# Strassen's seven products for the down projections of two MLPs, over all eight PSUM banks in turn

## The chip, the core and the metric

The kernel runs on one NeuronCore of a Trainium2 chip, as one launch. The metric is the device time of that launch in microseconds (us), the median of several runs. Engines are named as in the profile: PE (TensorE, the matrix engine), PEld (its weight loads), DVE (VectorE), ACT (ScalarE), POOL (GpSimd), SP (SyncE, which issues the loads of weights).

## What is computed

Two transformer-like blocks on one sequence of 1024 tokens with 1024 channels, in float32. What the change touches is the MLP at the end of each block:

```
u = rmsnorm(h, norm_mlp_g[l]) @ w_up[l]
h = h + jnp.square(jax.nn.relu(u)) @ w_down[l]
```

`w_up` is 1024 x 4096 and `w_down` 4096 x 1024. The second block has the same MLP with weights of its own, and a norm behind it that ends the kernel. The rest (dilated attention and a convolution, cross attention to 256 memory rows, a gated linear recurrence, neighbourhood attention) is the same before and after.

## The kernel before

All activations lie transposed, channels on the 128 partitions: `H` is 8 blocks of 128 channels x 1024 tokens. A float32 product is made of three passes of a faster 4-byte format: each operand is split into a high part that the format holds exactly and a low remainder, and hi*hi, hi*lo and lo*hi are summed in PSUM. PE's `job(q, s, x)` (L420) is one output block of 128 channels x 1024 tokens: for 8 inner blocks k, three passes, two halves of 512 tokens, 48 matmuls of 128x512, all recorded at L435. It fills `PJ[s]`, two of the eight PSUM banks; `PX` (four banks) is used by norms and attention, and stands unused in the MLPs. Job number 2q+s counts through the whole program, `s` alternating; semaphore `products` counts finished jobs.

The weights of a job come as one 512 KB tile into `raw[:, s]` by SP (`load`, L277). POOL's `split(q, s)` waits until the tile is there and until job 2q+s-2 has ended (its slot of `w_hi`/`w_lo` is then free), runs a one-column operation (L360), copies the high part (`w_hi`, L361) and subtracts for the low part (`w_lo`, L366), and raises `w_split`, for which PE waits at the job's start and SP before it loads the slot again. DVE empties the bank pair: in an up job with the ReLU and the norm's scale into `T[s]` (L1559), in a down job by an addition to `H` (`take`, L1284); either raises `free[s]`, for which PE waits two jobs on.

In an MLP, 32 up jobs make 32 inner blocks of 128, and the down projection needs all of them for each of 8 outputs. It goes in 4 chunks (`FF_CHUNKS`): 8 up jobs, then 8 down jobs over those 8 inner blocks. ACT squares `T[s]` twice, into the high part (L1076) and in place (L1077), and DVE subtracts for the low part (L1561). The chunks are hardware loops on PE, DVE, ACT and POOL. Ahead of the MLP, a norm: PE sums squares with `norm_stats` (L463) between the first two jobs, ACT takes the root (L878) and DVE the reciprocal `rstd` (`norm_std`, L1300), which the first eviction at L1559 needs. In the second MLP the last 8 down jobs are cut in halves of 512 tokens and written out by hand (L838), one bank for 24 matmuls, so that the last norm can begin early.

## Time and profile before

| | |
|---|---|
| median of 3 runs | 3181.73 us (3178.7 to 3182.39) |
| the profiled execution | 3180.11 us, its span 3178.3 us |
| PE busy | 3104.9 us, 98% of the span, 14982 matmuls |
| DVE / POOL / ACT busy | 43% / 33% / 25% |
| granted TensorE clock, mean | 0.994 |
| DMA | 61 GB/s over the span |
| the chain that ended last | PE 88%, of it L435 72% |

The span is cut into groups of instructions by line; a line of the chain of waits says what ended last at each moment. Matmuls overlap in the records, so that the mean duration of one (390 ns) is longer than the distance from one to the next; that distance is read from long pieces of the chain.

### The profile page before, as it was taken

How to read it: one execution, taken by the hardware profiler on the slowest of the kernel's cores; microseconds unless marked ns; L12 is line 12 of the kernel's file. 1: busy time of each engine (PE TensorE's matmuls, PEld its weight loads, DVE VectorE, ACT ScalarE, POOL GpSimd, SP SyncE). 2: the span in 40 equal slices, each digit the busy share in tenths (PEclk: the TensorE clock that was granted, in tenths of full speed). 3: DMA queues.
4: the chain of work that ended last, by engine and by line, in shares of the span. 5: the costliest groups of instructions: out<-in, count | busy, mean ns of one | idle time of the engine just before them, and what ended most of it. 6: DMA issues, size and time to landing. Idle time of an engine off the chain costs nothing.

```text
span 3178.3 us, 39032 instructions
## 1 busy us (share of the span) xinstructions
PE 3104.9 (98%) x14982; PEld 2464.2 (78%) x14982; DVE 1358.6 (43%) x1391; ACT 791.0 (25%) x1113; POOL 1052.2 (33%) x879
## 2 busy tenths in 40 slices
PE   8999999998999999999999999999999999999997
PEld 6776677875888888888767777887678888888886
DVE  7988874435331211113556566123775311111124
ACT  3005772114220101002243534112642201011011
POOL 3333323330333333333323333333353333333350
PEclk9999999999999999999999999999999999999999
DMA  3110002130111111111312121423131111111121
GB/s 138 47 40 33 2 28 86 47 119 7 47 46 47 53 47 46 53 46 46 112 50 80 61 74 53 165 71 130 37 126 47 46 53 47 47 50 50 46 67 53
DMA packets 50074, 194.16 MB, mean 61 GB/s; under 512 B 5680, under 2 KB 6320, under 8 KB 48560
## 3 DMA queue, kind: packets, MB, share of 16 engines
q1 hardware_dynamic: 43776, 152.50, 15.2%
q10 hardware_dynamic: 6192, 40.14, 3.3%
q8 instruction: 80, 1.31, 0.2%
q14 instruction: 26, 0.21, 0.0%
HBM read 171.12 MB, written 21.50 MB: 61 GB/s over the span
## 4 chain that ended last, share of the span: by engine, by line
PE 88%; DVE 7%; DMA 1%; ACT 1%; issue 1%; POOL 1%; SPq 0%; ACTq 0%; DVEq 0%; POOLq 0%
PE psum L435 72%; PE psum L838 3%; DVE cacc L1313 2%; PE psum L710 2%; PE psum L532 2%; PE psum L518 2%; PE psum L547 2%; DMA raw<-weights 1%; PE psum L771 1%; PE psum L785 1%; PE psum L758 1%; PE psum L661 1%; PE psum L641 1%; PE psum L497 0%; DVE rstd L1300 0%
## 5 line engine op out<-in xcount | busy, mean ns | idle before, releaser
L435 PE MATMUL psum<-A_hi,w_hi 128*128 128x512 f32 x2176 | 680.4, 394 | 18.3 <-DVE A_lo L1290 13.2
L435 PE MATMUL psum<-A_lo,w_hi 128*128 128x512 f32 x2176 | 671.5, 390 | 0.0
L435 PE MATMUL psum<-A_hi,w_lo 128*128 128x512 f32 x2176 | 671.0, 389 | 0.0
L360 POOL TENSOR_TENSOR small<-ident 128x1 f32<-128x1 f32 x250 | 63.0, 252 | 1813.3 <-PE psum L435 1781.9
L366 POOL TENSOR_TENSOR w_lo<-raw,w_hi 128x1024 fp32r<-128x1024 f32 x234 | 591.8, 2529 | 19.5
L435 PEld LDWEIGHTS psum<-A_hi,w_hi 128*128 128x128 f32 x2176 | 408.4, 188 | 113.5 <-issue 27.4
L435 PEld LDWEIGHTS psum<-A_lo,w_hi 128*128 128x128 f32 x2176 | 409.4, 188 | 85.5
L435 PEld LDWEIGHTS psum<-A_hi,w_lo 128*128 128x128 f32 x2176 | 409.1, 188 | 85.7
L435 PE MATMUL psum<-B_hi,w_hi 128*128 128x512 f32 x1472 | 454.9, 390 | 3.1 <-POOL w_lo L366 2.0
L435 PE MATMUL psum<-B_hi,w_lo 128*128 128x512 f32 x1472 | 453.2, 389 | 0.0
L435 PE MATMUL psum<-B_lo,w_hi 128*128 128x512 f32 x1408 | 433.6, 389 | 0.0
L1284 DVE TENSOR_TENSOR H<-psum,H 128x1024 f32 x80 | 98.0, 1225 | 562.2 <-PE psum L435 561.4
L435 PEld LDWEIGHTS psum<-B_hi,w_hi 128*128 128x128 f32 x1472 | 276.0, 188 | 62.4 <-POOL w_lo L366 2.4
L435 PEld LDWEIGHTS psum<-B_hi,w_lo 128*128 128x128 f32 x1472 | 276.3, 188 | 57.6
L435 PEld LDWEIGHTS psum<-B_lo,w_hi 128*128 128x128 f32 x1408 | 264.3, 188 | 54.9
L361 POOL TENSOR_SCALAR w_hi<-raw 128x1024 fp32r<-128x1024 f32 x250 | 264.4, 1058 | 0.0
L1559 DVE SCALAR_TENSOR_TENSOR t<-psum,rstd 128x1024 f32<-128x1024 f32 x64 | 78.4, 1225 | 374.7 <-PE psum L435 373.5
L1313 DVE SCALAR_TENSOR_TENSOR cacc<-U,par,cacc 128x1009 f32<-128x1009 f32 (+14 forms) x120 | 173.7, 1448 | 3.3
L1076 ACT ACTIVATE A_hi<-t 128x1024 f32 x32 | 34.0, 1062 | 531.9 <-DVE t L1559 531.9
L1076 ACT ACTIVATE B_hi<-t 128x1024 f32 x32 | 34.0, 1062 | 531.9 <-DVE t L1559 531.9
L384 POOL TENSOR_SCALAR P<-P,small 128x1024 f32<-128x1024 f32 x64 | 72.0, 1138 | 128.3 <-DVE small L1405 128.3
L1284 DVE TENSOR_TENSOR t<-psum,rstd 128x1024 f32<-128x1024 f32 x38 | 46.5, 1225 | 120.9 <-PE psum L435 117.2
(237 smaller groups left out, 3025.1 us busy)
## 6 DMA issues: line engine op xcount, KB each, us to landing
raw<-weights SPq DMA_DIRECT2D x256, 512.0 KB, 3.5
gate_spill<-RU SPq DMA_DIRECT2D x16, 512.0 KB, 3.1
H<-x ACTq DMA_DIRECT2D x2, 2048.0 KB, 8.6
x_spill<-H ACTq DMA_DIRECT2D x1, 4096.0 KB, 11.1
R<-gate_spill ACTq DMA_DIRECT2D x8, 512.0 KB, 4.5
mixed_spill<-t ACTq DMA_DIRECT2D x8, 512.0 KB, 2.9
BE<-rel_bias ACTq DMA_DIRECT2D x8, 512.0 KB, 4.4
MIX<-mixed_spill ACTq DMA_DIRECT2D x1, 4096.0 KB, 15.3
```

Of the source, the lines that this page charges most:

```text
L361: hi = pool.tensor_scalar(w_hi[:, s], raw[:, s], 1.0, 1.0, ALU.mult, ALU.mult)
L366: pool.tensor_tensor(w_lo[:, s], raw[:, s], f32(w_hi[:, s]), ALU.subtract).then_inc(S["w_split"], 1)
L384: pool.tensor_scalar(probs[:], probs[:], rsums[p % 3][:, h:h + 1], 1.0, ALU.mult, ALU.mult).then_inc(S["probs"], 1)
L435: last = pe.matmul(PJ[s][:, c:c + step], w[:, s, k, :], b[:, k, c:c + step], start=(k == 0 and i == 0), stop=(k == kblocks - 1 and i == 2))
L518: last = pe.matmul(to[h][:, c:c + HALF], Q[rows, m, P * t:P * t + P], K[rows, m, c:c + HALF], start=True, stop=True)
L532: last = pe.transpose(PX[:, HALF * (part % 2) + P * k:HALF * (part % 2) + P * k + P], P1[h][p % 3][:, key:key + P], ident[:])
L547: last = pe.matmul(PX[DH * h:DH * h + DH, 1024 + P * t:1024 + P * t + P], V[:, k, 2 * DH * m + DH * h:2 * DH * m + DH * h + DH], PT1[h][p ...
L838: last = pe.matmul(fin_bank(n), w, x[:, k, half_of(h)], start=(k == 0 and i == 0), stop=(k == KB - 1 and i == 2))
L1076: tallies["u_hi"](act.activation(block_of(u[0], m), T[s][:], ACT.Square))
L1284: dve.tensor_tensor(out, PJ[s], in1, op).then_inc(free[s], 1)
L1313: done(dve.scalar_tensor_tensor(cacc[:, a:b], u(a + sh, b + sh), w, cacc[:, a:b], ALU.mult, ALU.add))
L1559: dve.scalar_tensor_tensor(T[s][:], PJ[s], 0.0, rstd[:], ALU.max, ALU.mult).then_inc(free[s], 1)
```

## The change

In each MLP, 24 of the 32 inner blocks (6 groups of 4) go through the down projection by Strassen's scheme, in the form with seven products. Its blocks are: two output blocks 2j and 2j+1, two halves of the group's inner blocks (two blocks each), and two halves of 512 tokens. One new unit `("down", g, j)`, a *pair* in what follows, is 7 products of 6 matmuls (2 inner blocks x 3 passes) where the plain way needs 48 matmuls; each group has 4 pairs. Each product fills one bank of its own, and DVE adds the seven banks to `H` in six additions (`add_pair`), which raise `st_read` or `free`; PE waits for these before it fills a bank again. `H` is changed to differences of its blocks at the MLP's start and back at the end of the pairs (`rebase`, two operations on 4x512 columns each time). The last 8 inner blocks go the plain way.

The operands of the products: DVE and ACT make seven activations per two inner blocks, each in a high and a low part (`combine` on DVE, `split_group` on ACT; into `XS`, which lies where the squared activations lay). DVE makes four sums of weights per pair (`weight_sums`, 4 operations on 256 columns), into one buffer `WS`; POOL splits the three weight quarters that are used as they are (`split_pair`) and then `WS`. The order of the units is the table `FF_UNITS`: four up jobs; then per group two up jobs, four pairs, two up jobs (u u d d d d u u); up jobs 26 to 31; the 8 plain down jobs. The unit count stays 64. All of it is straight-line code but the last down jobs of the first MLP. POOL also waits for the norm's sums before it splits unit 2, since some of its new buffers lie in `acc`.

The core of the diff (the low parts of the last 8 blocks, the table of weights made on the host and the semaphores' names are left out):

```diff
+GROUPS = 6
+def ff_units():
+    units = [("up", t) for t in range(4)]
+    for g in range(GROUPS):
+        units += [("up", 4 * g + 4), ("up", 4 * g + 5)] + [("down", g, j) for j in range(4)]
+        if g < GROUPS - 1:
+            units += [("up", 4 * g + 6), ("up", 4 * g + 7)]
+    return units + [("up", t) for t in range(26, 32)] + [("last", m) for m in range(KB)]
+FF_UNITS = ff_units()
...
+        XS = [at(f"XS{l}", (o_b, o_a)[l], [7, 2, 2, HALF], F32R) for l in range(2)]
...
+        WS = at("WS", o_t + 2 * KIB4, [KB, P])
...
-            splits(ROUNDS["xo"], ROUNDS["qkv2"] + 6)
+            def split_pair(q, s, layer):
+                pool.wait_ge(raw_in[s], 16 * q + 16)
+                pool.wait_ge(S["products"], 2 * q + s - 1)
+                pool.tensor_tensor(small[:, 12:13], ident[:, 0:1], ident[:, 0:1], ALU.mult)
+                hi12, lo12 = W12[layer][s]
+                hi22, lo22 = W22[layer][s]
+                chain(pool.tensor_scalar(hi12[:], raw[:, s, 0:4], 1.0, 1.0, ALU.mult, ALU.mult))
+                chain(pool.tensor_scalar(hi22[:], raw[:, s, 6:8], 1.0, 1.0, ALU.mult, ALU.mult))
+                chain(pool.tensor_tensor(lo12[:], raw[:, s, 0:4], f32(hi12[:]), ALU.subtract))
+                chain(pool.tensor_tensor(lo22[:], raw[:, s, 6:8], f32(hi22[:]), ALU.subtract))
+            def split_units(name, layer, end):
+                pool.wait_ge(S["stats"], 3 + 2 * layer)
+                pairs = 0
+                for at_unit in range(2, end):
+                    unit, q, s = FF_UNITS[at_unit], ROUNDS[name] + at_unit // 2, at_unit % 2
+                    if unit[0] != "down":
+                        split(q, s)
+                        continue
+                    split_pair(q, s, layer)
+                    pairs += 1
+                    pool.wait_ge(S["st_weights"], 4 * GROUPS * layer + pairs)
+                    chain(pool.tensor_scalar(w_hi[:, s], WS[:], 1.0, 1.0, ALU.mult, ALU.mult))
+                    pool.tensor_tensor(w_lo[:, s], WS[:], f32(w_hi[:, s]), ALU.subtract).then_inc(S["w_split"], 1)
+            splits(ROUNDS["xo"], ROUNDS["ff"])
+            split(ROUNDS["ff"], 0)
+            split(ROUNDS["ff"], 1)
+            split_units("ff", 0, len(FF_UNITS))
+            splits(ROUNDS["rec_in"], ROUNDS["qkv2"] + 6)
...
+            def fast_down(q, s, layer, g, j):
+                pair = 4 * GROUPS * layer + 4 * g + j
+                wait_split(pe, q, s, "late")
+                if j == 0:
+                    pe.wait_ge(S["st_lo"], 2 * GROUPS * layer + 2 * g + 2)
+                w12, w22 = W12[layer][s], W22[layer][s]
+                sums = (w_hi[:, s], w_lo[:, s])
+                def product(bank, w, at_w, x):
+                    for i in range(2):
+                        for t, (a, b) in enumerate(((0, 0), (0, 1), (1, 0))):
+                            last = pe.matmul(bank, w[a][:, at_w + i, :], XS[layer][:, x, b, i, :],
+                                             start=(i == 0 and t == 0), stop=(i == 1 and t == 2))
+                    return last
+                if pair > 1:
+                    pe.wait_ge(S["st_read"], 3 * pair - 5)
+                product(PX[:, HALF * (j % 2):HALF * (j % 2) + HALF], w12, 0, 0).then_inc(S["st_done"], 1)
+                if pair:
+                    pe.wait_ge(S["st_read"], 3 * pair - 1)
+                product(PX[:, 1024:1024 + HALF], w12, 2, 1)
+                product(PX[:, 1024 + HALF:2048], sums, 2, 6).then_inc(S["st_done"], 1)
+                if j == 0:
+                    pe.wait_ge(free[0], q)
+                else:
+                    pe.wait_ge(S["st_read"], 3 * pair)
+                product(PJ[0][:, 0:HALF], sums, 4, 4).then_inc(S["st_done"], 1)
+                product(PJ[0][:, HALF:SEQ], w22, 0, 5).then_inc(S["st_done"], 1)
+                pe.wait_ge(free[1 - s], q + s)
+                product(PJ[1][:, 0:HALF], sums, 6, 2)
+                product(PJ[1][:, HALF:SEQ], sums, 0, 3).then_inc(S["products"], 1)
             def mlp(name, x, u, n, layer):
                 q0 = ROUNDS[name]
-                u_ready = lambda c: (S["u_lo"], [8 * c + (32 * layer + k + 1) for k in range(KB)])
-                rounds(q0, 4, x, stats=norm_stats(n), ready=norm_ready(n))
-                rounds(q0 + 4, 4, u, ready=u_ready(0))
-                with pe.Fori(1, FF_CHUNKS - layer) as c:
-                    for i in range(4):
-                        for s in range(2):
-                            job(8 * c + (q0 + i), s, x)
-                    for i in range(4):
-                        for s in range(2):
-                            job(8 * c + (q0 + 4 + i), s, u, ready=u_ready(c) if i == 0 and s == 0 else None)
+                job(q0, 0, x, ready=norm_ready(n))
+                norm_stats(n)()
+                for at_unit in range(1, len(FF_UNITS) - 8):
+                    unit, q, s = FF_UNITS[at_unit], q0 + at_unit // 2, at_unit % 2
+                    if unit[0] == "up":
+                        if FF_UNITS[at_unit - 1][0] == "down":
+                            pe.wait_ge(S["st_read"], 3 * (4 * GROUPS * layer + 4 * FF_UNITS[at_unit - 1][1] + 4))
+                        job(q, s, x)
+                    else:
+                        fast_down(q, s, layer, *unit[1:])
+                if layer == 0:
+                    rounds(q0 + 28, 4, u, ready=(S["u_lo"], [k + 1 for k in range(KB)]))
...
+                def split_group(c):
+                    i = c % 2
+                    x = XS[layer]
+                    at_h = lambda p: x[:, p:p + 2, 0, i, :]
+                    halves = lambda t: t[:].rearrange("p (a b) -> p a b", a=2)
+                    tallies["st_hi"](act.activation(x[:, 0, 0, i, :], T[0][:, 0:HALF], ACT.Copy))
+                    tallies["st_hi"](act.activation(at_h(1), halves(T[1]), ACT.Copy))
+                    for t in range(2):
+                        act.wait_ge(S["st_sum"], 4 * GROUPS * layer + 2 * c + t + 1)
+                        tallies["st_hi"](act.activation(at_h(3 + 2 * t), halves(T[t]), ACT.Copy))
...
+                def combine(c):
+                    i = c % 2
+                    left, right = slice(0, HALF), slice(HALF, SEQ)
+                    halves = lambda t: t[:].rearrange("p (a b) -> p a b", a=2)
+                    minus = lambda out, a, b: chain(dve.tensor_tensor(out, a, b, ALU.subtract))
+                    done = 4 * (2 * GROUPS * layer + c)
+                    dve.wait_ge(S["st_hi"], done + 1)
+                    dve.tensor_tensor(x[:, 0, 1, i, :], T[0][:, left], f32(x[:, 0, 0, i, :]), ALU.subtract)
+                    dve.wait_ge(S["st_hi"], done + 2)
+                    chain(dve.tensor_tensor(x[:, 1:3, 1, i, :], halves(T[1]), f32(x[:, 1:3, 0, i, :]), ALU.subtract))
+                    minus(T[0][:, left], T[0][:, right], T[0][:, left])
+                    tl["st_sum"](dve.tensor_tensor(T[0][:, right], T[1][:, right], T[0][:, right], ALU.subtract))
+                    minus(T[1][:, right], T[1][:, right], T[0][:, left])
+                    tl["st_sum"](dve.tensor_tensor(T[1][:, left], T[1][:, left], T[1][:, right], ALU.subtract))
+                    dve.wait_ge(S["st_hi"], done + 3)
+                    dve.tensor_tensor(x[:, 3:5, 1, i, :], halves(T[0]), f32(x[:, 3:5, 0, i, :]), ALU.subtract)
+                    dve.wait_ge(S["st_hi"], done + 4)
+                    tl["st_lo"](dve.tensor_tensor(x[:, 5:7, 1, i, :], halves(T[1]), f32(x[:, 5:7, 0, i, :]), ALU.subtract))
...
+                def weight_sums(g, j):
+                    at_unit = units_of[("down", g, j)]
+                    q, s = q0 + at_unit // 2, at_unit % 2
+                    dve.wait_ge(raw_in[s], 16 * q + 16)
+                    if 4 * g + j:
+                        before = units_of[("down", g, j - 1) if j else ("down", g - 1, 3)]
+                        wait_split(dve, q0 + before // 2, before % 2, "late")
+                    k = lambda a: raw[:, s, 2 * a:2 * a + 2]
+                    to = lambda a: WS[:, 2 * a:2 * a + 2, :]
+                    chain(dve.tensor_tensor(to(0), k(2), k(3), ALU.add))
+                    dve.tensor_tensor(to(2), k(0), k(2), ALU.subtract)
+                    chain(dve.tensor_tensor(to(1), to(0), k(0), ALU.subtract))
+                    tl["st_weights"](dve.tensor_tensor(to(3), k(1), to(1), ALU.subtract))
+                def add_pair(q, s, g, j):
+                    pair = 4 * GROUPS * layer + 4 * g + j
+                    both = lambda half: H[:, 2 * j:2 * j + 2, half_of(half)]
+                    banks = lambda t, n=2: t.rearrange("p (a b) -> p a b", a=n)
+                    dve.wait_ge(S["st_done"], 4 * pair + 1)
+                    twice = banks(PX[:, HALF * (j % 2):HALF * (j % 2) + HALF], 1).to_broadcast([P, 2, HALF])
+                    tl["st_read"](dve.tensor_tensor(both(0), twice, both(0), ALU.add))
+                    dve.wait_ge(S["st_done"], 4 * pair + 2)
+                    tl["st_read"](dve.tensor_tensor(both(0), banks(PX[:, 1024:2048]), both(0), ALU.add))
+                    for n in range(2):
+                        dve.wait_ge(S["st_done"], 4 * pair + 3 + n)
+                        out = H[:, 2 * j + 1, half_of(0)]
+                        chain(dve.tensor_tensor(out, PJ[0][:, half_of(n)], out, ALU.add))
+                    tl["st_read"](dve.tensor_tensor(both(1), both(1), banks(PJ[0]), ALU.subtract))
+                    wait_job(dve, q, s)
+                    dve.tensor_tensor(both(1), banks(PJ[1]), both(1), ALU.add).then_inc(free[s], 1)
+                def rebase(forward):
+                    even, odd = H[:, 0:KB:2, :], H[:, 1:KB:2, :]
+                    steps = [(even[:, :, HALF:SEQ], odd[:, :, HALF:SEQ]), (odd[:, :, HALF:SEQ], odd[:, :, 0:HALF])]
+                    for out, other in steps if forward else steps[::-1]:
+                        chain(dve.tensor_tensor(out, out, other, ALU.subtract if forward else ALU.add))
+                rebase(True)
+                for at_unit in range(len(FF_UNITS) - 8):
+                    unit, q, s = FF_UNITS[at_unit], q0 + at_unit // 2, at_unit % 2
+                    if unit[0] == "down":
+                        g, j = unit[1:]
+                        add_pair(q, s, g, j)
+                        if j < 2:
+                            weight_sums(g, j + 2)
+                        if j == 3:
+                            if g < GROUPS - 1:
+                                combine(2 * g + 2)
+                            else:
+                                dve.wait_ge(free[s], q + 1)
+                                rebase(False)
+                                low(0)
+                                low(1)
+                        continue
+                    t = unit[1]
+                    evict(q, s)
+                    if t < 4 * GROUPS:
+                        if t == 1 or t % 4 == 3:
+                            dve.wait_ge(S["st_sq"], 4 * GROUPS * layer + t + 1)
+                            combine(t // 2)
+                    elif t >= 4 * GROUPS + 2:
+                        low(t - 4 * GROUPS)
+                    if t >= 4 and t % 4 < 2 and t <= 4 * GROUPS + 1:
+                        weight_sums(t // 4 - 1, t % 4)
```

How the order of instructions moves, at three places. PE, a down job in the first MLP of before (the waits of an instruction in brackets; the first rows of 16 like them):

```order
L435 MATMUL psum<-B_hi,w_hi 128x512 [waits free1,w_split]
L435 MATMUL psum<-B_hi,w_hi 128x512
L435 MATMUL psum<-B_lo,w_hi 128x512 x2
L435 MATMUL psum<-B_hi,w_lo 128x512 x2
L435 MATMUL psum<-B_hi,w_hi 128x512 x2
```

The second pair of a group in the change, from its first row to the fourth product (`W_010` and `W_011` are a weight quarter's high and low part):

```order
L746 MATMUL psum<-XS_131,W_010_135 128x512 [waits w_split]
L746 MATMUL psum<-XS_131,W_010_135 128x512
L746 MATMUL psum<-XS_131,W_011_136 128x512
...
L746 MATMUL psum<-XS_131,W_010_135 128x512 [waits st_read]
...
L746 MATMUL psum<-XS_131,w_hi 128x512 [waits st_read]
...
L746 MATMUL psum<-XS_131,w_hi 128x512 [waits free0]
```

Where a job waited at its start alone, a pair also waits ahead of its second, fourth and sixth product. POOL, the work for one job of before:

```order
L360 TENSOR_TENSOR small<-ident 128x1 [waits products,raw1]
L361 TENSOR_SCALAR w_hi<-raw 128x1024
L366 TENSOR_TENSOR w_lo<-raw,w_hi 128x1024 [waits pool_chain]
```

And for one pair in the change:

```order
L420 TENSOR_TENSOR small<-ident 128x1 [waits products,raw1]
L423 TENSOR_SCALAR W_010_135<-raw 128x512
L424 TENSOR_SCALAR W_010_143<-raw 128x256 [waits pool_chain]
L425 TENSOR_TENSOR W_011_136<-raw,W_010_135 128x512 [waits pool_chain]
L426 TENSOR_TENSOR W_011_144<-raw,W_010_143 128x256 [waits pool_chain]
L439 TENSOR_SCALAR w_hi<-WS 128x1024 [waits st_weights,pool_chain]
L440 TENSOR_TENSOR w_lo<-WS,w_hi 128x1024 [waits pool_chain]
```

The old two stand at its end, behind DVE's sums (`st_weights`), and four new ones ahead of them. On DVE the six additions of a pair are one of 1024 columns behind the first product, one of 1024 behind the third, one of 512 behind the fourth and the fifth each, one of 1024 (which frees `PJ[0]`), and one of 1024 behind the last. In the first two pairs of a group the four sums for the pair after the next follow the sixth addition; behind the fourth pair comes `combine`. DVE at the start of the first MLP, before:

```order
L1296 TENSOR_TENSOR acc<-acc,t_61 128x1024 [waits norm_sq,norm_lo]
L112 REGISTER_ALU [waits norm_acc]
L112 COMPARE_AND_BRANCH
L1300 RECIPROCAL rstd<-rstd 128x1024 [waits std]
L112 UNCONDITIONAL_BRANCH [waits dve_chain]
L112 UNCONDITIONAL_BRANCH
L112 ISA
L1559 SCALAR_TENSOR_TENSOR t_59<-psum,rstd 128x1024 [waits products]
```

And in the change:

```order
L1409 TENSOR_TENSOR acc<-acc,t_61 128x1024 [waits norm_sq,norm_lo]
L128 REGISTER_ALU [waits norm_acc]
L128 COMPARE_AND_BRANCH
L1413 RECIPROCAL rstd<-rstd 128x1024 [waits std]
L1739 TENSOR_TENSOR H<-H 128x4x512 [waits dve_chain] x2
L1672 SCALAR_TENSOR_TENSOR t_59<-psum,rstd 128x1024 [waits products,dve_chain]
```

The two operations of `rebase` stand between the reciprocal and the first eviction, where before no work stood.

## Rows read from the trace of the kernel before

**Rows 1.** The page: each engine's busy time, share of the span, instructions

```profile
PE 3104.9 (98%) x14982; PEld 2464.2 (78%) x14982; DVE 1358.6 (43%) x1391; ACT 791.0 (25%) x1113; POOL 1052.2 (33%) x879
```

**Rows 2.** Chain that ended last: start us, us, what; MLPs, last down jobs

```profile
875.41 696.36 PE psum L435 x3072
...
2473.28 598.46 PE psum L435 x2640
...
3127.60 32.70 PE psum L838 x144
```

**Rows 3.** Busy by windows, first MLP: PE, PEld, DVE, ACT, POOL, clock, DMA

```profile
875.00:1571.00 696.00, 696.00 (x3071) 576.09 (x3071) 161.24 (x123) 97.82 (x105) 230.89 (x190) 1.00 0.16 50
```

**Rows 4.** Timeline of POOL in the first MLP: start us, us, what

```profile
887.77 3.25 POOL L366 TENSOR_TENSOR w_lo<-raw,w_hi 128x1024 fp32r<-128x1024 f32 x1
...
908.25 0.20 POOL L360 TENSOR_TENSOR small<-ident 128x1 f32<-128x1 f32 x1 [7.25 <-PE psum L435]
908.40 1.05 POOL L361 TENSOR_SCALAR w_hi<-raw 128x1024 fp32r<-128x1024 f32 x1
909.54 2.40 POOL L366 TENSOR_TENSOR w_lo<-raw,w_hi 128x1024 fp32r<-128x1024 f32 x1
```

**Rows 5.** Timeline of DVE at the first MLP's start

```profile
876.60 6.55 DVE L1300 RECIPROCAL rstd<-rstd 128x1024 f32<-128x1024 f32 x1 [7.60 <-ACT rstd L878]
883.66 1.23 DVE L1559 SCALAR_TENSOR_TENSOR t<-psum,rstd 128x1024 f32<-128x1024 f32 x1 [0.50 <-DVE rstd L1300]
887.34 1.42 DVE L1561 TENSOR_TENSOR B_lo<-t,B_hi 128x1024 f32 x1 [2.45 <-ACT t L1077]
888.88 1.23 DVE L1559 SCALAR_TENSOR_TENSOR t<-psum,rstd 128x1024 f32<-128x1024 f32 x1
```

**Rows 6.** Groups by line and shape: busy us, mean ns, idle before

```profile
L1765 DVE TENSOR_TENSOR H<-psum,H 128x512 f32<-128x512 f32 x16 | 11.1, 692 | 43.4 <-PE psum L838 43.3
L1699 DVE COPY PT<-psum 128x256 f32<-128x256 f32 x64 | 27.1, 423 | 7.9 <-PE psum L771 7.7
L401 POOL TENSOR_SCALAR P<-P,small 128x512 f32<-128x512 f32 x32 | 21.8, 695 | 44.9 <-DVE small L1691 44.9
L1077 ACT ACTIVATE t<-t 128x1024 f32<-128x1024 f32 x64 | 68.1, 1063 | 2.0
```

**Rows 7.** DVE's evictions from PSUM: count, ns min/median/max, first and last start

```profile
L1284 DVE TENSOR_TENSOR H<-psum,H x80: 1224/1225/1225, 486.1 to 2984.8; 128x1024 f32 x80
...
L1559 DVE SCALAR_TENSOR_TENSOR t<-psum,rstd x64: 1224/1225/1226, 883.7 to 3071.8; 128x1024 f32<-128x1024 f32 x64
```

**Rows 8.** Timeline of POOL behind the second attention

```profile
2340.11 3.44 POOL L366 TENSOR_TENSOR w_lo<-raw,w_hi 128x1024 fp32r<-128x1024 f32 x1
```

**Rows 9.** Timeline of DVE, same stretch

```profile
2340.06 1.23 DVE L1740 TENSOR_TENSOR t<-t,MIX 128x1024 f32<-128x1024 f32 x1
2341.32 3.30 DVE L1732 TENSOR_TENSOR A_lo<-t,A_hi 128x1024 fp32r<-128x1024 f32 x1
```

**Rows 10.** Timeline of PE after a wait of 2.48 us

```profile
487.45 1.19 PE L435 MATMUL psum<-A_hi,w_hi 128*128 128x512 f32 x2 [2.48 <-DVE H L1284]
488.44 1.05 PE L435 MATMUL psum<-A_lo,w_hi 128*128 128x512 f32 x2
489.29 1.05 PE L435 MATMUL psum<-A_hi,w_lo 128*128 128x512 f32 x2
```

**Rows 11.** Busy by windows: after that wait, and after one of 5.0 us

```profile
487.00:490.00 3.00, 2.55 (x6) 2.10 (x7) 1.40 (x2) 2.30 (x3) 1.77 (x1) 0.55 0.15 19
...
3076.00:3126.00 50.00, 49.70 (x220) 40.82 (x219) 16.33 (x20) 5.71 (x9) 22.35 (x12) 1.00 0.18 53
```

**Rows 12.** Chain: the wait of 5.0 us that ended at 3076.78

```profile
3059.94 11.80 PE psum L435 x52
...
3076.78 49.96 PE psum L838 x219
```

More of the change, by code:

```diff
@@ L814, in _ @@
             mlp("ff2", B, A, 4, 1)
-            for i in range(4):
-                for s in range(2):
-                    job(LAST - 4 + i, s, B)
             for n in range(2 * KB):
@@ L831, in _ @@
                     if n == 0:
[L832 removed]
+                        pe.wait_ge(S["u_lo"], KB + k + 1)
                     if m < 2:
@@ L1563, in mlp, with evict @@
[L1563 to L1568 removed]
+                x = XS[layer]
+                sums_made = [0]
+                def evict(q, s):
+                    wait_job(dve, q, s)
+                    dve.scalar_tensor_tensor(T[s][:], PJ[s], 0.0, rstd[:], ALU.max, ALU.mult).then_inc(free[s], 1)
```

79 lines of the change are left out of this document (49 added, 30 removed).

## The prediction, written before the changed kernel was run

> **What bounds the kernel now.** I read the page first: PE is busy for 3104.9 of 3178.3 us [rows 1], so only fewer or shorter matmuls, or the few gaps, can make this kernel faster. Then the chain that ended last: the first MLP stands in it as one unbroken piece, 3072 matmuls in 696.36 us; the second, up to its last down jobs, as 2640 in 598.46 us [rows 2]. Both give 0.2267 us from one matmul to the next, job changes, loop ends and waits included. So a job of 48 is 10.88 us and six matmuls are 1.36 us. The windows show how far the others are from binding there: in 696 us DVE works 161, ACT 98, POOL 231 [rows 3]. POOL's work for a job is 0.20 + 1.05 + 2.40 us with gaps of 0.09, 3.8 us of 10.88, and begins when the job two back has ended [rows 4].
>
> **What the change removes.** A pair has 42 matmuls where 48 stood: 6 x 48 pairs = 288 fewer, x 0.2267 = **-65.3 us**. All of it lies on PE's path, since nothing else ends last in either MLP [rows 2]. The kernel has no other row for this count; the pair's matmuls have the same shape, and each its own weight load, as before (PE and PEld have the same count [rows 1]). The Trainium skill (TensorE: Matmul & The Clock Gate, "Back-to-back issue gap") gives 512/2.4 + 2.5 ns, 216 ns, for such a matmul at full clock. By it the saving would be 62.2 us; this trace has 226.7 ns for the 4-byte format, and I use that.
>
> **A bank for each six matmuls.** The nearest row is the written-out end of the second MLP, one bank per 24 matmuls: 144 in 32.70 us [rows 2], 0.05 us more than 144 x 0.2267 for six bank changes. At 0.008 us each, 336 products would cost 2.8 us. A job change in the loops costs nothing. I take 0, and keep 2.8 for the range; it also bounds what straight-line code costs against loops.
>
> **POOL, the closest margin.** For the second, third and fourth pair of a group it has 7 x 1.36 = 9.52 us, from the start of the pair before. Its ordinary pieces: 0.20; one-source operations of 512 and 256 columns at 0.70 [rows 6] and, on the line through 0.70 and 1.05 for 1024 [rows 4], 0.52; two-source ones on the line from 0.20 (1 column) to 2.40 (1024), 1.30 and 0.75; then WS at 1.05 + 2.40. With six gaps of 0.09 that is 7.5 us. DVE's four sums (256 columns, 0.43 each by [rows 6], 1.7 us) come 1.3 to 2 us after the start and must be done before WS is split. They have both inputs in SBUF, and such a DVE operation and POOL's exclude one another: at 2340 us DVE's operation runs its normal 1.23, POOL's takes 3.44 in place of 2.40, and DVE's next, queued behind it, 3.30 [rows 8, 9]; the same at 887 us, with 3.25 on POOL [rows 4, 5]. If nothing at all overlaps, 7.5 + 1.7 = 9.2 us: still 0.3 us before PE needs it. I put the likely end at 8.8 to 9.0 and the cost at **0**. The first pair of a group is made beside an up job (10.88 us) and has more room; an up job's 3.8 us fits anywhere.
>
> **DVE.** A pair's additions are 4 x 1.23 + 2 x 0.69 = 6.3 us [rows 6, 7] of 9.52. None of them is stretched by POOL: an operation with one PSUM input never took more than 1.226 us [rows 7], also at 888.88, in the middle of POOL's stretched one [rows 4, 5]. With the sums in front (done at about 5.2) the additions of the second and third pair end 11.5 us after their pair's start, that is 2.0 us into the next. PE needs `PX` again 1.36 us into the next pair (read at 7.7), `PJ[0]` 4.1 us in (read at 10.3, 0.8 in) and `PJ[1]` 6.8 us in. So every bank is free in time: **0**. The fourth pair has no sums before its additions, so the up job behind it finds `PJ[0]` read. `combine` with its ACT part is a chain of 1.23 (eviction) + 1.06 (square) + 1.66 (copies) + 1.23 + 4 x 0.69 + 1.06 + 1.23 = 10.2 us [rows 6, 7] against up jobs of 10.88; POOL may stretch it by 1 to 2.4 us. What is late then is the next eviction, and PE wants that bank only 10.88 us later: 0. Per group of 81.6 us DVE has 51 us, POOL 45, ACT 12. The slots of `raw` are filled again after `w_split`, some 9 us before they are read; SP's queue has nothing new in it.
>
> **The start of each MLP.** The reciprocal ends at 883.15 and the first eviction began at 883.66 [rows 5]. PE finishes the second job 10.88 us after 875.41, at 886.29, and its third needs the eviction's end (884.9 before, so no wait). `rebase` puts two operations of 2048 columns ahead of it: on the line through 0.69 for 512 and 1.23 for 1024 some 2.3 each [rows 6, 9]. First eviction over at 883.2 + 4.6 + 1.3 = 889.1: PE waits 2.8 us, twice **+5.6 us**. Lower bound 0 (if PE's order had more slack than I see), upper 2 x (2.8 + 1.0 for one of them held up by POOL). A wait can also halve the clock: after one of 2.48 us, in a stretch with others, the granted clock was 0.55 over 3 us and the distance 0.425 us [rows 10, 11], costing eight matmuls 0.2 each; after one of 5.0 us behind dense work it stayed 1.00 [rows 11, 12]. The MLP's start is dense, like the second: 0, with 2 x 1.6 in the range. `rebase` back (4.6 us) lies beside up job 26, and POOL's wait for the norm's sums delays the split of unit 2 by 1.7 us of some 7 spare: both 0.
>
> **The sum.** -65.3 + 5.6 = -59.7. The profiled execution took 3180.1 us around its span of 3178.3, so 3120.4; the median shown is 1.6 above it: **3122.0 us**.
>
> **Rivals.** (a) POOL is late. For: the margin is 0.3 to 0.7 us, and its small operations have no rows. Against: even the sum without any overlap fits. If a pair's weights come 0.4 to 1.1 us late, 36 pairs (three per group) cost 14 to 40 us: 3136 to 3162.
> (b) DVE is late: its sums wait behind several of POOL's operations, WS's 2.40 us among them, and the additions behind them run over. A wait of 1 to 2 us in two pairs per group, 24 pairs, costs 24 to 48 us: 3146 to 3170. Against: `PJ[0]` has 3.3 us to spare.
> (c) It gets slower: PE pauses briefly at the product changes, each with a wait and a fresh bank, and the clock falls. Place: the 2016 matmuls of the pairs. Price: 0.425 - 0.2267 = 0.198 us for each at half clock [rows 10]. It decides from 59.7 / 0.198 = 302 of them, 15% or six per pair; eight per pair, as in rows 10, would be 76 us: 3198. Against: 64 jobs with a wait at each lost nothing [rows 2]. The Trainium skill names just this (the same page, "A second HAM failure mode: psum-queue depth-cycling"): cycling through banks lets PE idle briefly between groups and its clock swing between the two levels. By that rule the change would lose its gain; the trace has no bank cycling this fast, so it can't refute it.
> (d) The saving isn't there. The order of instructions has 42 matmuls per pair, so I give this nothing of its own.
>
> **How the numbers follow.** Forecast 0.74, (a) 0.13, (b) 0.05, (c) 0.05; 0.03 is left for what I don't see. About 0.2% (6 us) is what a measurement here can tell from no change. The forecast, (a) and (b) are all faster: 0.92; (c) makes 0.05 slower; the rest lies between. Range: low end, no wait at the MLPs' start and a little noise, 3181.7 - 65.3 - 1 = 3115. The forecast's own costs reach to 3122.0 + 2.8 + 2.0 + 3.2 = 3130; the range goes on through most of (a), to 3150.
>
> **What would show it.** Each pair 9.5 us on PE; no wait of PE for `w_lo` or for an addition to `H` inside the pairs; two waits near 2.8 us for DVE at the third job of each MLP; clock at 1.00; WS's low part over some 0.5 us before the pair starts. Waits for L440 speak for (a), waits for L1723 to L1732 for (b), a clock below 1 in the MLPs' windows for (c). The forecast is wrong if PE's chain in the MLPs has gaps of more than 10 us together.

## The result, and the profile of the changed kernel

The change takes 3123.02 us in the median of 4 runs (3119.3 to 3126.63), beside 3181.14 us for the kernel before (4 runs, 3178.7 to 3182.39). The ratio is 0.9818, 95% interval 0.9801 to 0.9835: 58 us faster, and 1 us from the forecast of 3122. The terms behind the forecast were not all of that quality, as the rows show.

The page of the changed kernel: its span, each engine's busy time with the share of the span and the instructions, the granted clock in 40 slices, and the two largest of its three groups of the new products. They answer to [rows 1].

```profile
span 3117.5 us, 38588 instructions
...
PE 3039.6 (98%) x14694; PEld 2411.0 (77%) x14694; DVE 1906.4 (61%) x1975; ACT 830.9 (27%) x1161; POOL 1213.1 (39%) x1071
...
PEclk9999999999999999999999999999999999999999
...
L746 PE MATMUL psum<-XS,w_hi 128*128 128x512 f32 x768 | 236.4, 389 | 0.0
...
L746 PE MATMUL psum<-XS,W 128*128 128x512 f32 x864 | 211.4, 389 | 0.0
```

288 matmuls are gone (14982 to 14694). That PE's busy time fell by 65.3 us (3104.9 to 3039.6), just the first term, is in part chance. In the first MLP it fell by 30.8 us (696.4 to 665.6), in the second, up to its last down jobs, by 30.7 (598.4 to 567.7), since the slow restart described below takes back 1.9 us of each saving; the other 3.8 us lie where the change does nothing. The first term is read from the chain below. DVE's share rose from 43% to 61% and POOL's from 33% to 39%, and the last column of the products' groups says what that cost PE: its idle time before them is 0.0. So PE still bounds the kernel, and the question is where the other 5 to 7 us of the 65 went.

The chain that ended last in the changed kernel, first MLP (start us, us, what), answers to [rows 2]:

```profile
870.89 1.73 PE psum L517 x4
...
872.65 1.12 ACT rstd L964
...
873.80 6.56 DVE rstd L1413
...
880.38 2.30 DVE H L1739
...
882.71 2.30 DVE H L1739
...
885.04 1.23 DVE t L1672
...
886.41 45.41 PE psum L489 x192
931.81 38.08 PE psum L746 x168
969.89 43.52 PE psum L489 x192
...
1377.89 163.20 PE psum L489 x720
```

Read it from the end. Six groups of four pairs take 38.08 us each, 9.52 us a pair, and 38.08 / 168 = 0.2267 us a matmul: waits and bank changes of the pairs cost nothing that can be read. The up projections between them are at 43.52 / 192, again 0.2267. One piece differs: the first 192 matmuls take 45.41 us. Ahead of them stands what the single piece of [rows 2] did not have: the chain leaves PE and goes through the norm on ACT and DVE, the two halves of the rebase (L1739) and the first eviction (L1672), before PE goes on at 886.41. PE waits there, once in each MLP. Its waits (us in all, how many, longest):

```profile
PE psum L489 <- DVE t L1672: 5.7, 2, 2.9
```

Two stretches of the first MLP by engine (PE, PEld, DVE, ACT, POOL, then the granted clock, the DMA share and GB/s):

```profile
886.40:1541.00 654.60, 654.59 (x2881) 541.88 (x2882) 421.68 (x411) 116.91 (x128) 306.74 (x283) 1.00 0.16 53
...
887.00:890.00 3.00, 3.00 (x10) 2.35 (x9) 1.08 (x2) 2.87 (x4) 1.54 (x1) 0.64 0.06 8
```

From the wait to the MLP's end PE is busy without a break. Just behind the wait, from 887 to 890 us, the granted clock is 0.64: part of that time TensorE ran at 1.2 GHz in place of 2.4, and the 192 matmuls cost 45.41 - 43.52 = 1.9 us more. Behind the same wait at full clock, which three runs below show, they take 43.80 us; so 1.6 us of the 1.9 are the clock's and 0.3 us belong to the restart. One start thus costs 2.9 + 1.9 = 4.8 us, the second MLP's too (45.40 us for its first 192), 9.5 us together.

The account of the two profiled executions, 3180.1 against 3119.3 us, -60.8: the first MLP went from 696.36 to 668.47 us (872.62 to 1541.09), -27.9 = -32.6 + 4.8. The second MLP and what follows it gave -28.2, the same sum with 0.3 us of noise. The remaining -4.7 us lie ahead of the first MLP (its norm sums end at 872.62, before at 875.41) and between the MLPs (901.5 to 899.6), where the change does nothing; the experiments show this scatter too.

### The profile page after: what moved, and what is told of

The parts are those of the page before. It is cut to its first block, busy times and chain, and to the rows that moved or that the text cites. A ratio compares the mean times of both kernels' runs of the same rounds, so it can differ in the third digit from the quotient of the medians.

```text
span 3117.5 us, 38588 instructions
## 1 busy us (share of the span) xinstructions
PE 3039.6 (98%) x14694; PEld 2411.0 (77%) x14694; DVE 1906.4 (61%) x1975; ACT 830.9 (27%) x1161; POOL 1213.1 (39%) x1071
## 4 chain that ended last, share of the span: by engine, by line
PE 87%; DVE 8%; ACT 2%; issue 1%; DMA 1%; POOL 1%; SPq 0%; ACTq 0%; DVEq 0%; POOLq 0%
PE psum L489 56%; PE psum L746 15%; PE psum L924 3%; DVE cacc L1426 2%; PE psum L799 2%; PE psum L572 2%; PE psum L586 2%; PE psum L601 2%; PE psum L860 1%; PE psum L874 1%; PE psum L847 1%; PE psum L715 1%; DVE rstd L1413 1%; DMA raw<-weights 1%; PE psum L695 1%
## 5 line engine op out<-in xcount | busy, mean ns | idle before, releaser
L489 PE MATMUL psum<-A_hi,w_hi 128*128 128x512 f32 x1792 | 562.9, 395 | 21.7 <-DVE A_lo L1403 13.6
L489 PE MATMUL psum<-A_lo,w_hi 128*128 128x512 f32 x1792 | 553.5, 390 | 0.0
L489 PE MATMUL psum<-A_hi,w_lo 128*128 128x512 f32 x1792 | 553.1, 390 | 0.0
L489 PEld LDWEIGHTS psum<-A_hi,w_hi 128*128 128x128 f32 x1792 | 336.6, 189 | 102.3 <-issue 30.7
L489 PE MATMUL psum<-B_hi,w_hi 128*128 128x512 f32 x1088 | 337.8, 392 | 4.5 <-DVE t L1672 2.9
L489 PE MATMUL psum<-B_hi,w_lo 128*128 128x512 f32 x1088 | 335.5, 390 | 0.0
L489 PE MATMUL psum<-B_lo,w_hi 128*128 128x512 f32 x1024 | 315.8, 390 | 0.0
L1672 DVE SCALAR_TENSOR_TENSOR t<-psum,rstd 128x1024 f32<-128x1024 f32 x64 | 78.2, 1224 | 265.5 <-PE psum L489 263.9
L746 PE MATMUL psum<-XS,w_hi 128*128 128x512 f32 x768 | 236.4, 389 | 0.0
L746 PE MATMUL psum<-XS,W 128*128 128x512 f32 x864 | 211.4, 389 | 0.0
L746 PEld LDWEIGHTS psum<-XS,W 128*128 128x128 f32 x864 | 162.2, 188 | 33.6
L746 PEld LDWEIGHTS psum<-XS,w_hi 128*128 128x128 f32 x768 | 144.2, 188 | 29.9
```

The source lines that it names most:

```text
L489: last = pe.matmul(PJ[s][:, c:c + step], w[:, s, k, :], b[:, k, c:c + step], start=(k == 0 and i == 0), stop=(k == kblocks - 1 and i == 2))
L746: last = pe.matmul(bank, w[a][:, at_w + i, :], XS[layer][:, x, b, i, :], start=(i == 0 and t == 0), stop=(i == 1 and t == 2))
L1672: dve.scalar_tensor_tensor(T[s][:], PJ[s], 0.0, rstd[:], ALU.max, ALU.mult).then_inc(free[s], 1)
```

## Experiments

Each was timed in 3 or 5 rounds beside the kernel before; ratios are against the runs of before on the same chip. Its medians there were 3179.91 us (beside c0, e1, e3 and e4), 3179.5 us (beside e2, e5, e6 and e7) and 3181.77 us (beside e8 and e1b). The base c0 belongs to the first group, so that a difference from it in another group also holds what the kernel before differs by, 0.4 us for the second.

### The change again, as the base (c0)

> The change again, unaltered, as the measure for the others of this group. Theory: a median near 3123 us, as before (288 matmuls fewer, -65.3, and two waits at the starts of the MLPs with the clock's fall behind them, +9.6). Rival, that the first result was luck by a part of its 7 us scatter: outside 3119 to 3127.

Measured: 3124.81 us (3120.65 to 3126.73), ratio 0.9824 (0.9811 to 0.9838). Both MLPs' first 192 matmuls took 45.4 us again.

### The rebase later (e1)

```diff
-                rebase(True)
                 for at_unit in ...
...
                     t = unit[1]
                     evict(q, s)
+                    if t == 2:
+                        rebase(True)
```

> The forward rebase (two operations of 2048 columns on DVE) stands behind the third eviction in place of ahead of the first. Theory: the wait of PE for the first eviction goes (2.9 us at each MLP) and with it the fall of the clock behind it (the first 192 matmuls took 45.4 us, not 43.5): 2 x 4.8 = 9.6 us faster than the change, 3113 to 3114 us. Rival 1, the clock falls for another reason: only 2 x 2.9 = 5.8 us, and the pieces of 192 stay at 45.4. Rival 2, something else ends at the same time (the second eviction, combine): less than 3 us.

Measured: 3112.07 us (3111.22 to 3115.47), ratio 0.9789 (0.9776 to 0.9802), 12.7 us below the base. The chain of this kernel, first MLP:

```profile
872.16 54.45 PE psum L489 x240
926.60 38.08 PE psum L746 x168
```

and DVE's timeline in the same place (start us, us, what):

```profile
895.21 6.68 DVE L1739 TENSOR_TENSOR H<-H 128x2048 f32<-128x2048 f32 x2
```

The 240 matmuls behind the norm's sums, five jobs, are one piece, 54.45 us; in the change the same ones took 931.81 - 872.62 = 59.19. That is 4.74 us for the first MLP, and 4.75 for the second (its first 240 take 54.44). The rebase itself is as long as before, beside matmuls: its 6.68 us for two operations, stretched by POOL, now cost nothing. Both starts give 9.5 us, and so do the spans of the two profiled executions (3118.9 and 3109.4 us). The other 3 us between the medians stand in no kept trace. The granted clock from 887 to 890 us is 1.00.

### The seventh product twice (e2)

```diff
-                product(PJ[1][:, HALF:SEQ], sums, 0, 3).then_inc(S["products"], 1)
+                product(PJ[1][:, HALF:SEQ], sums, 0, 3)
+                product(PJ[1][:, HALF:SEQ], sums, 0, 3).then_inc(S["products"], 1)
```

> Each pair issues its seventh product twice (the second run of six matmuls starts the bank anew, so the sum is the same): 48 matmuls per pair, as the plain way has, with all of the change's banks, waits, sums and additions. It gives the price of the matmuls alone. Theory: 288 x 0.2267 = 65.3 us slower than the change, 3188 to 3190 us, no wait inside the pairs. Rival, the pairs are paced by DVE or POOL and PE's matmuls hide behind them: clearly less than 65 us.

Measured: 3184.94 us (3184.45 to 3190.74, 10 runs), ratio 1.0019 (1.0009 to 1.0029), 60.1 us above the base and 5 us above the kernel before. The chain shows four pairs as the same piece as four up jobs:

```profile
934.12 43.52 PE psum L746 x192
```

So with eight products in place of seven the whole gain is gone, as the theory has it, and what is left is the price of the MLPs' starts. But 60.1 is not 65.3. The chains place the difference: the two MLPs are 32.6 and 32.4 us longer than the base's (701.08 against 668.45 us, and 602.94 against 570.56 up to the last down jobs), while the two profiled executions differ by 70.0 us and the medians by 60.1. The scatter is outside the MLPs and in their starts. Since the starts scatter (below), the same pair was run without them.

### The rebase later, with and without an eighth product (e8, e1b)

The two edits above together, and the first alone again.

> The rebase moved behind the third pair's eviction of the next up projection, as in e1_rebase_later, and every pair of down tiles issues its seventh product twice, so that the down projections have the 8 products of the kernel before on the banks and the order of the change. 48 pairs x 6 matmuls x 0.2267 us = 65.3 us above e1_rebase_later. Theory (a matmul left out is worth its full 0.2267 us, and the 61 us between e2_eighth_product and the change was 65.3 less a scatter of the two MLP starts): 65.3 +- 1 us above e1_rebase_later, about 3177 us, within 0.2% of the kernel before, and less scatter than e2_eighth_product had. Rival (the pairs' products cost less than 0.2267 us each beside the others, or an eighth product covers a wait that the seven leave open): 61 us above, about 3173 us.

> The kernel of e1_rebase_later again, on the chip and beside the runs of e8_later_eighth: 3112 us by both theories, 2.1% below the kernel before, with no wait at the MLPs' third job.

Measured: 3179.6 us (3177.57 to 3183.51, 10 runs), ratio 0.9997 (0.9987 to 1.0006), and 3115.86 us (3113.89 to 3116.61, 4 runs), ratio 0.9792 (0.9776 to 0.9809). The medians are 63.7 us apart, between the two theories, but the chains leave no doubt. With eight products:

```profile
876.15 54.44 PE psum L489 x240
930.59 43.52 PE psum L746 x192
...
1409.31 163.20 PE psum L489 x720
```

With seven:

```profile
875.40 54.45 PE psum L489 x240
929.85 38.08 PE psum L746 x168
...
1375.93 163.20 PE psum L489 x720
```

The first MLP is 696.36 us with eight (876.15 to 1572.51), to the hundredth what [rows 2] have for the kernel before, and 663.72 us with seven (875.40 to 1539.12; 663.72 in the earlier run as well). The difference is 32.64 us, and the second MLP gives 32.6 again: 65.3 us in all. All else that the change brought, with the rebase moved, costs PE's path nothing. The scatter is elsewhere: the first MLP began at 872.16 in one run and at 875.40 us in the other of the same kernel.

### POOL's margin: one, two and four more operations (e3, e4, e5)

The low part of the four weight tiles (L425) is computed once, twice or four times more for each pair, with the same output. The edit for one more:

```diff
                 chain(pool.tensor_tensor(lo22[:], raw[:, s, 6:8], f32(hi22[:]), ALU.subtract))
+                chain(pool.tensor_tensor(lo12[:], raw[:, s, 0:4], f32(hi12[:]), ALU.subtract))
```

> POOL makes one low part of 512 columns twice in each pair's split (1.35 to 1.45 us more). It tells how wide POOL's margin is. In the change WS's low part ends 8.0 us after POOL's start and PE needs it at 9.4; 0.9 us of that start-to-end is a wait for DVE's sums. Theory of a margin of 1.4 us: the added operation takes up the wait and holds DVE's last sum up by about 1 us, the end moves to 9.0 to 9.1, PE waits for nothing, 0 us (within 3). Rival, the margin is as small as the prediction said (0.3 to 0.7): PE waits 0.3 to 0.7 us in 36 pairs, 10 to 25 us slower than the change.

> The same with two added operations per pair. Theory: the end moves by 1.0 + 1.4 = 2.4 us to 10.4 to 10.5, about 1.1 us behind PE's need, in the 36 pairs that are prepared beside another pair; none in the 12 that are prepared beside an up job. 40 us slower than the change if the clock stays full; waits named for the low part of WS (L440). Rival (c) of the prediction, short pauses bring the clock down: further 0.2 us for each matmul at half clock, 1.6 us per pause as at the MLP's start, near 100 us slower in all and a granted clock clearly under 0.99. Rival, POOL catches up: under 20 us.

> POOL with four added operations of 512 columns per pair, so that PE pauses for some 3.9 us ahead of each of 36 pairs and 2.4 us ahead of the 12 first ones. (Two added ones made pauses of 1.0 us, and the granted clock stayed at 0.99 to 1.00.) Theory, a pause of this length between dense stretches costs only itself: 36 x 3.9 + 12 x 2.4 = 170 us slower than the change, near 3293 us, clock 0.99. Rival (c) in its long form, each pause of more than about 3 us is followed by a stretch at half clock, as at the MLPs' start (1.6 to 1.9 us): a further 48 x 1.6 = 77 us, near 3370 us, and clock near 0.96 or less in the MLPs.

Measured: with one more 3124.33 us (0.9827, 0.9812 to 0.9842), a median no different from the base's; with two 3161.12 us (0.9934, 0.9919 to 0.9949), +36.3; with four 3280.52 us (1.0308, 1.0291 to 1.0326), +156.

The chain with one more shows what its median hides, from the first start to the first group's end:

```profile
886.12 43.80 PE psum L490 x192
929.92 19.09 PE psum L747 x84
949.04 19.40 PE psum L747 x84
968.43 43.52 PE psum L490 x192
```

The group takes 38.51 us in place of 38.08, and the two MLPs lose 2.7 us each against the change at the same clock, 5.4 in all. The weight loads wait for POOL's `w_lo` at 23 places, about two a group, with no wait at the matmuls recorded. The median doesn't show it; in the profiled execution 1.6 us came back because the clock stayed up behind the first start (43.80 us in the first line). So the theory of no wait fell a little, and the rival's 10 to 25 us are too much.

PE's waits for POOL with two more:

```profile
PE psum L748 <- POOL w_lo L442: 25.0, 36, 0.9
```

Thirty-six waits, three per group, as rival (a) had them, 0.5 us each in front of one pair of a group and 0.7 to 0.9 in front of the two others. They show 25.0 us, while the time rose by 36.3: each pause costs some 0.3 us more than the idle time that stands at it. Half of that is how the records count: a matmul's record is 0.39 us long while the next one follows after 0.2267, so that idle time begins 0.16 us after the next matmul was due. The granted clock from 931 to 1013 us, over the pauses of the first group, is 1.00. So the cost begins right behind the change: with one more operation POOL ends 9.1 to 9.5 us after the pair's start, where PE wants its work after 9.52.

With four more operations the pauses are longer, and the clock moves. Five restarts after such a pause (timeline of PE; in brackets the idle time before and what ended it):

```profile
933.59 4.33 PE L750 MATMUL psum<-XS,W 128*128 128x512 f32 x12 [2.06 <-POOL w_lo L444]
...
946.27 3.01 PE L750 MATMUL psum<-XS,W 128*128 128x512 f32 x12 [1.25 <-POOL w_lo L444]
...
959.17 4.46 PE L750 MATMUL psum<-XS,W 128*128 128x512 f32 x12 [3.08 <-POOL w_lo L444]
...
1065.99 3.01 PE L750 MATMUL psum<-XS,W 128*128 128x512 f32 x12 [3.06 <-POOL w_lo L444]
...
1441.05 5.49 PE L750 MATMUL psum<-XS,W 128*128 128x512 f32 x12 [3.06 <-POOL w_lo L444]
```

Twelve matmuls need 3.0 us at full clock. Of the 45 pauses the 12 of 1.8 us or less were all followed by twelve matmuls in 3.0 us; of the 12 of 2.05 or 2.06 us four were not (4.2 to 4.6 us), and of the 21 of 2.8 to 3.1 us eighteen were not (4.3 to 5.5 us). After 3.06 us they took 5.49 us once and 3.01 another time. The pauses were shorter than I had expected (2.06, 1.25, 3.08 and some 1.4 us in a group). The excess of 156 us is 104 us of waits, and the rest restarts and the lower clock: the windows over the two MLPs have 0.97 and 0.96.

### DVE: one more operation per pair (e7)

One eviction of 1024 columns is done twice (the first time with its product taken times zero), with the same output.

```diff
                     wait_job(dve, q, s)
+                    chain(dve.scalar_tensor_tensor(both(1), banks(PJ[1]), 0.0, both(1), ALU.mult, ALU.add))
                     dve.tensor_tensor(both(1), banks(PJ[1]), both(1), ALU.add).then_inc(free[s], 1)
```

> DVE does one more operation of 1024 columns per pair (it adds PJ[1] times zero to H, 1.25 us, ahead of the last addition). It tells DVE's margin, for rival (b). DVE's round in a pair with sums is 9.58 us in the change, against PE's 9.52. Theory: DVE falls behind by 1.3 us in each of two pairs; PJ[0]'s and WS's slack takes the first and most of the second, and PE waits 1.4 us or so once or twice per group: 15 to 35 us slower than the change. Rival, DVE has room to spare: 0 (within 3). Other rival, every pair is paced by DVE: 48 x 1.3 = 62 us.

Measured: 3120.88 us (3119.45 to 3125.86), ratio 0.982 (0.9803 to 0.9836): nothing, where the theory had 15 to 35 us. That theory fell. DVE's timeline in this kernel, second pair, the second and third of the four sums:

```profile
942.30 0.84 DVE L1712 TENSOR_TENSOR WS<-raw 128x256 f32<-128x256 f32 x1
943.06 0.41 DVE L1713 TENSOR_TENSOR WS<-WS,raw 128x256 f32<-128x256 f32 x1
```

and in the changed kernel, where all 48 pairs have them as long (a mean of 1.38 and 0.97 us):

```profile
933.53 1.41 DVE L1712 TENSOR_TENSOR WS<-raw 128x256 f32<-128x256 f32 x1
934.86 0.96 DVE L1713 TENSOR_TENSOR WS<-WS,raw 128x256 f32<-128x256 f32 x1
```

In the change the four sums take 3.2 us from start to end (933.06 to 936.28), since two of them meet POOL's operations: each of the two ends 0.3 us behind the operation that it met (POOL's L425 ends at 934.65, L426 at 935.53), and POOL's keep their usual length. With the extra one the sums come later in a pair that follows a pair, only one of them meets a POOL operation, the short L426, and they take 2.15 us (941.78 to 943.93). Of the 1.23 us added 1.07 are won back. The first pair of a group keeps its 3.2 us.

### Four banks in place of eight (e6)

The products go through `PJ` alone, and each waits until the bank that it takes has been read (cut; the additions on DVE read from there too):

```diff
-                product(PX[:, HALF * (j % 2):HALF * (j % 2) + HALF], w12, 0, 0).then_inc(S["st_done"], 1)
-                if pair:
-                    pe.wait_ge(S["st_read"], 3 * pair - 1)
-                product(PX[:, 1024:1024 + HALF], w12, 2, 1)
-                product(PX[:, 1024 + HALF:2048], sums, 2, 6).then_inc(S["st_done"], 1)
...
+                product(PJ[0][:, HALF:SEQ], w12, 0, 0).then_inc(S["st_done"], 1)
+                pe.wait_ge(free[1 - s], q + s)
+                product(PJ[1][:, 0:HALF], w12, 2, 1)
+                product(PJ[1][:, HALF:SEQ], sums, 2, 6).then_inc(S["st_done"], 1)
+                product(PJ[0][:, 0:HALF], sums, 4, 4).then_inc(S["st_done"], 1)
+                pe.wait_ge(S["st_read"], 3 * pair + 1)
+                product(PJ[0][:, HALF:SEQ], w22, 0, 5).then_inc(S["st_done"], 1)
+                pe.wait_ge(S["st_read"], 3 * pair + 2)
+                product(PJ[1][:, 0:HALF], sums, 6, 2)
```

> The pairs use PJ's four banks alone: the first product goes to PJ[0]'s right bank, the second and third to PJ[1], the fourth to PJ[0]'s left bank; the fifth then waits for the first addition, the sixth for the second one. It undoes the part of the change that its title names. Theory by DVE's times in the change (first addition over 5.7 us after the pair's start where sums stand ahead, fifth product wanted at 5.44): 0.3 us per pair in 36 pairs, 10 to 12 us slower than the change, 3133 to 3137 us. Rival, eight banks carry the gain: one addition's length or more per pair, over 45 us slower.

Measured: 3150.4 us (3146.98 to 3152.13), ratio 0.9906 (0.9889 to 0.9923), 26 us above the base; neither theory's number. The chain of this kernel, first pair of a group and on:

```profile
934.19 1.36 PE psum L746 x6
935.55 0.03 issue
935.57 4.37 PE psum L746 x18
...
939.95 5.78 PE psum L746 x24
```

Eighteen matmuls after a bank that was just read take 4.37 us, not 4.08, and 24 take 5.78, not 5.44, with hardly a wait shown. PE does wait there: the fifth product, due at 939.79 us, begins at 939.95, behind the end of the first addition at 939.89. The wait is about as long as the 0.16 us by which two matmuls' records overlap, so that it doesn't show as idle time of PE. It shows at the weight loads (what the products' line waited for: us, times):

```profile
  DVE H L1721: 15.8, 37
  DVE H L1730: 15.7, 36
  DVE t L1670: 5.4, 12
```

One of the 37 is PE's own wait of 0.2 us; the other 84 places, at 0.3 us each, are the loss. The theory had only the fifth product's wait for the first addition (L1721), 36 times; the second product's wait for the last addition of the pair before (L1730) or for the eviction before (L1670) doubles it. A group of four pairs is 40.3 to 40.5 us here, 38.08 in the change; twelve times some 2.3 us are the 26 to 28. So taking all eight banks in turn is worth some 26 us of the gain; with four of them half of it would have come.

## Why the prediction was right, point by point

**"288 fewer, x 0.2267 = -65.3 us."** Right: the MLPs with seven and eight products differ by 2 x 32.6 us in the chain. By the 216 ns of the Trainium skill (TensorE: Matmul & The Clock Gate, "Back-to-back issue gap") it would have been 62.2; the prediction doesn't say that the section calls this the gap of an isolated matmul and has 131 ns for a stream with weight loads, by which I estimate 37.7 us. The trace agrees with neither: 38.08 us for 168 is 226.7 ns.

**"A bank for each six matmuls ... 0."** Right: 0.2267 us with the bank changes in it. The 0.008 us per change from the nearest row was an upper bound only.

**"POOL, the closest margin."** The sign was right, the size not. The price of POOL's small operations in the changed kernel (groups by line and shape: busy us, mean ns):

```profile
L425 POOL TENSOR_TENSOR W<-raw,W 128x512 fp32r<-128x512 f32 x48 | 66.8, 1391 | 4.0
...
L439 POOL TENSOR_SCALAR w_hi<-WS 128x1024 fp32r<-128x1024 f32 x48 | 50.6, 1054 | 43.1 <-DVE WS L1714 43.1
...
L426 POOL TENSOR_TENSOR W<-raw,W 128x256 fp32r<-128x256 f32 x48 | 38.4, 801 | 3.8
...
L423 POOL TENSOR_SCALAR W<-raw 128x512 fp32r<-128x512 f32 x48 | 29.7, 619 | 0.2 <-issue 0.2
...
L424 POOL TENSOR_SCALAR W<-raw 128x256 fp32r<-128x256 f32 x48 | 19.6, 409 | 4.0
```

I had 0.70, 0.52, 1.30 and 0.75 us for L423 to L426, they took 0.62, 0.41, 1.39 and 0.80. With the waits WS's low part ended 8.2 to 8.4 us after the pair's start in the three pairs of the first group that have a pair behind them, 1.2 to 1.4 before PE needed it, not "8.8 to 9.0": I had added DVE's four sums to POOL's time as if POOL stood still for them. Two of them do meet POOL's operations, but there it is DVE that waits (3.2 us for sums of 1.7), and POOL's own run on at their usual length. POOL's only loss to DVE is the 43.1 us ahead of L439 (0.90 a pair), when it waits for the sums. POOL's timeline of the first pair, which PE began at 931.81, and the start of the next:

```profile
936.43 1.06 POOL L439 TENSOR_SCALAR w_hi<-WS 128x1024 fp32r<-128x1024 f32 x1 [0.90 <-DVE WS L1714]
937.57 2.41 POOL L440 TENSOR_TENSOR w_lo<-WS,w_hi 128x1024 fp32r<-128x1024 f32 x1
941.48 0.19 POOL L420 TENSOR_TENSOR small<-ident 128x1 f32<-128x1 f32 x1 [1.50 <-PE psum L746]
```

One more operation of 1.4 us uses the margin up (5.4 us lost in all) and a second one comes at its full price, which bears out a margin of 1.2 to 1.4 us and refutes the one of 0.3 to 0.7.

**"DVE ... 0."** Right, with the sums over at 4.5 us (5.2 predicted) and the additions at 10.95 us (11.5). What POOL stretched are sums: L1712 took 1.41 us where 0.43 is the undisturbed time, while the additions, with one input from PSUM, stayed at 1.22 to 1.23 beside the same POOL operations. That is as the Trainium skill has it (SBUF — State Buffer, "Who interferes with whom": DVE and GpSimd share one port pair, under an exclusive lock; with at most one input in SBUF such a DVE instruction doesn't take part), and the trace agrees.

**"The start of each MLP, +5.6."** The step whose size was off. The waits were as worked out, 2.87 us each (2.8). The clock was taken at 0 because the MLP's start was "dense, like the second", with 2 x 1.6 us in the range; it fell, and cost just 2 x 1.6. The restart behind each wait, 2 x 0.3, was not in the sum. The starts are 9.5 us in place of 5.6. Dense work before and behind the pause does not keep the clock up: the eight profiled kernels with the rebase in front have sixteen such starts, all with a pause of 2.9 us. In thirteen the clock fell (45.2 to 45.4 us for 192 matmuls, where these are one piece of the chain; with four more POOL operations 1.9 and 3.1 us were lost over the first 144); in three it stayed, all in the first MLP (43.8 us; with one and two more POOL operations, and with the one more on DVE). The wait of 5.0 us behind which it stayed at 1.00 [rows 11, 12] was the exception, and I had made it the rule. Measured by terms the sum is -65.3 + 9.5 = -55.8 or 3125.9 us from the median shown; the base's 3124.8 and the first result's 3123.0 lie 1 to 3 us below it, within the scatter that the traces show outside the MLPs. The forecast of 3122 was partly lucky: 3.9 us that it left out and that scatter nearly cancelled.

**"`rebase` back ... and POOL's wait ... both 0", `combine` 0.** Right; no piece of the chain within the MLPs is on DVE, POOL or ACT behind the start. `rebase` back took 6.69 us in place of 4.6, beside a POOL operation, and nothing waited for it.

**Rival (a)** is real but 1.2 to 1.4 us of POOL's time away; priced at 14 to 40 us, it came to 5.4 with 1.4 us of added work and to 36.3 with 2.8. **Rival (b)** was not reached with one more operation of 1.23 us. **Rival (c)**: the product changes alone, each with a fresh bank, left the granted clock at 1.00. The Trainium skill's rule of falling clocks when PE cycles through banks ("A second HAM failure mode: psum-queue depth-cycling") did not bite here, even with 36 real pauses of 0.5 to 0.9 us added; what lowered the clock was pauses of 2 to 3 us, at the MLPs' starts and with four more operations. **(d)** is refuted by the eighth product.

## What to carry to other kernels

Where an engine stands in the chain as one unbroken piece, an instruction less is worth its distance to the next one, and a doubled one shows it in the chain to the hundredth while medians blur it by some microseconds. The gain can be lost in two quiet places: the first wait that new work puts before a producer (here a rebase ahead of an eviction, cured by issuing it three evictions later, 9.5 us), and the banks (26 us). A median can hide several microseconds of waits that the chain shows (5.4 us with one more POOL operation). By these runs a pause of 2.8 to 3.1 us should be priced with the clock as likely to fall, one of 2 us with a chance of it, and every pause with about 0.3 us on top of the idle time shown.

## What the runs showed of the hardware

- The best kernel of this study is the change with the rebase moved: 3112.07 and 3115.86 us, ratio 0.9789 (0.9776 to 0.9802) and 0.9792.
- A pause of 2.9 us amid dense matmuls lowered the granted clock in 13 of 16 cases, in the second MLP in all eight; with four more POOL operations the restart was slow after 18 of 21 pauses of 2.8 to 3.1 us, 4 of 12 of 2.05 or 2.06 us and none of 12 of 1.8 us or less. What decides it between equal pauses stays open; no experiment varied that alone.
- A pause costs some 0.3 us beyond the idle time at it, even where the clock stays: the first 192 matmuls took 43.80 us in place of 43.52 in the three starts at full clock, 36 pauses of 25.0 us cost 36.3, and with four banks PE loses 0.3 us at each of 84 places where DVE's read ends just too late, with next to no idle time of PE recorded. Of the 0.3 us 0.16 are the overlap of two matmuls' records (0.39 us long, 0.2267 apart); what the rest is stays open.
- DVE's operations on two SBUF inputs are stretched to 1.41 and 0.96 us where they meet POOL's, which keep their length (1.35 and 0.80), and a delay of DVE by 1.2 us makes them shorter (0.84 and 0.41). With one input from PSUM they stay at 1.22 to 1.23 us.
